# A raw query weight outside the row slots, two last expert rows weighed one by one, and an earlier second head in the last mixer

## What is computed

```
ue = peer_u[experts]
ve = peer_v[experts]
act = jax.nn.gelu(jnp.einsum('td,thkd->thk', hc, ue).astype(jnp.float32), approximate=False)
return jnp.einsum('thk,thkd->td', (g * act).astype(ve.dtype), ve)
```

```
m = jnp.maximum(jnp.max(s, axis=-1, keepdims=True), sink)
e = jnp.exp(s - m)
p = e / (jnp.sum(e, axis=-1, keepdims=True) + jnp.exp(sink - m))
o = jnp.einsum('bnkgqp,bnpkd->bnqkgd', p.astype(vb.dtype), vb)
```

## Time and profile before

| | |
|---|---|
| runs of the kernel, us | 1650.83, 1653.07, 1652.2: median 1652.2 |
| the profiled execution, us | 1650.42, its span 1648.6 |
| mean granted TensorE clock | 0.981 |
| busy share of the span | PE 91%, weight loads 66%, DVE 68%, ACT 46%, POOL 17% |
| the chain that ended last | PE 64%, DMA 18%, DVE 11%, ACT 4% |
| DMA | 443 MB, of which 268 MB are the expert rows |

### The profile page before, as it was taken

How to read it: one execution, slowest core, us unless ns; L and a number is a source line. 1 busy time by engine, 2 the same in 40 slices (tenths; PEclk the granted TensorE clock), 3 DMA queues, 4 the chain that set the end, 5 groups by cost and what they waited for, 6 DMA issues and landing times.

```text
span 1648.6 us, 18823 instructions
## 1 busy us (share of the span) xinstructions
PE 1504.9 (91%) x6882; PEld 1090.7 (66%) x6882; DVE 1121.2 (68%) x2054; ACT 753.4 (46%) x1401; POOL 284.3 (17%) x317
## 2 busy tenths in 40 slices
PE   7999999999789889788798777879999999899999
PEld 6899888888644444344353332338888889788887
DVE  6669666666877766767866876458666566866654
ACT  5444553344434444334443433235555347655532
POOL 0000000000243333334433334313000002000000
PEclk9999999999999999999999999999999999999999
DMA  6754544554599999999999999984455554135563
GB/s 241 269 179 157 176 154 153 179 181 162 217 419 421 421 421 420 421 421 409 422 421 421 403 422 421 404 346 144 153 188 195 186 198 135 52 131 195 186 191 116
DMA packets 73356, 443.04 MB, mean 269 GB/s; under 512 B 7047, under 2 KB 9359, under 8 KB 29872
## 3 DMA queue, kind: packets, MB, share of 16 engines
q0 software_dynamic: 36864, 268.45, 39.4%
q1 hardware_dynamic: 32672, 165.69, 29.6%
q10 hardware_dynamic: 3728, 7.70, 1.3%
HBM read 440.75 MB, written 2.63 MB: 269 GB/s over the span
## 4 chain that ended last, share of the span: by engine, by line
PE 64%; DMA 18%; DVE 11%; ACT 4%; issue 2%; POOL 0%; SPq 0%; DVEq 0%; ACTq 0%; POOLq 0%
PE banks L1410 24%; DMA arena<-experts,xn 18%; PE banks L1845 11%; PE banks L1433 11%; PE banks L1438 6%; DVE arena L2474 3%; PE banks L1320 3%; PE banks L1733 2%; DVE w_lo L2037 2%; PE banks L1552 1%; PE banks L1575 1%; ACT xn L1010 1%; PE banks L1344 1%; ACT xn L1014 1%; PE banks L1501 1%
## 5 line engine op out<-in xcount | busy, mean ns | idle before, releaser
L1845 PE MATMUL banks<-arena,xn 128*128 128x512 f32 x1024 | 499.1, 626 | 108.5 <-ACT xn L1014 108.2
L2037 DVE TENSOR_TENSOR w_lo<-raw,w_hi 128x2048 fp32r<-128x2048 f32 x152 | 348.0, 2290 | 198.4 <-PE banks L1410 100.5
L2474 DVE CUSTOM_DVE_ANT_0 arena<-arena,banks 128x1024 f32<-128x1024 f32 x256 | 311.7, 1218 | 191.9 <-DMA arena<-experts,xn 191.5
L1845 PEld LDWEIGHTS banks<-arena,xn 128*128 128x128 f32 x1024 | 188.7, 197 | 343.4 <-issue 172.9
L717 ACT ACTIVATE w_hi<-raw 128x2048 fp32r<-128x2048 f32 x152 | 291.1, 1918 | 234.2 <-PE banks L1410 145.7
L652 POOL DMA_INDIRECT arena<-experts,xn x256 | 252.0, 984 | 421.5 <-PE banks L1845 388.3
L1410 PE MATMUL banks<-w_hi,op 128*128 128x512 f32 x1152 | 292.7, 393 | 1.4 <-DVE op L2671 0.8
L1410 PEld LDWEIGHTS banks<-w_hi,op 128*128 128x128 f32 x1152 | 216.5, 189 | 47.7 <-issue 2.1
L1003 ACT ACTIVATE xn<-xn,stat 128x2 f32<-128x2 f32 x128 | 37.8, 295 | 378.9 <-DVE xn L2474 378.8
L1433 PE MATMUL banks<-op,w_hi 128*128 128x512 f32 x792 | 200.4, 393 | 0.0
L1433 PEld LDWEIGHTS banks<-op,w_hi 128*128 128x128 f32 x792 | 141.8, 189 | 25.9 <-issue 1.1
(11 more groups left out here) (277 smaller groups left out, 1371.6 us busy)
## 6 DMA issues: line engine op xcount, KB each, us to landing
raw<-wstream SPq DMA_DIRECT2D x152, 1024.0 KB, 5.4
arena<-experts,xn POOLq DMA_INDIRECT x256, 12.7
xn<-mem_in ACTq DMA_DIRECT2D x2, 1024.0 KB, 6.4
arena<-wstream SPq DMA_DIRECT2D x2, 1024.0 KB, 7.9
scratch<-scratch ACTq DMA_DIRECT2D x1, 1536.0 KB
x<-x_in SPq DMA_DIRECT2D x2, 512.0 KB, 4.8
arena<-scratch ACTq DMA_DIRECT2D x1, 1024.0 KB, 7.3
raw<-keys_in SPq DMA_DIRECT2D x1, 1024.0 KB, 4.7
```

The source lines that it names most:

```text
L1845: mm = pe.matmul(sums[:, n, :], diag[:, s, :], rows[:, s, D + n * CW:D + (n + 1) * CW], start=(at == 0), stop=(at == PAIRS - 1), skip_grou ...
L2037: dve.tensor_tensor(w_lo[:, n % LO, :, :], slot_of(n), w_hi[:, n % HI, :, :].bitcast(F32), ALU.subtract).then_inc(lo_ready, 1)
L2474: dve.tensor_tensor_reduce(u, u, token_rows[k // PAIRS][:, :, :], 1.0, 0.0, ALU.mult, ALU.add, dots[:, s:s + 1]).then_inc(dot_ready, 1)
```

## The change

There are five edits.

1. The fourth `pq` half is loaded into `memkv`, a buffer of 128x2048 that is `memk` and `memv` in one, which hold nothing until later. Only the third half lies in a row slot, the last. So row 6 waits for no low part, and row 7 for that of the third half instead of the fourth.
2. `weigh_rows` can weigh a single row; the last two rows, 254 and 255, are weighed one by one.
3. `add_rows(1)` begins its first half when the first of the last row's two products is done (`last_sum`), its second half when the row is.
4. In `swa` the second item is normalised directly after the first, and the low parts of both `outb` halves follow it, ahead of the maxima of the third item. `take_inverses(2)` and `memory_inverses` no longer make low parts.
5. Normalisation of the first `memb` head stands ahead of the last `take` of `swa`.

ACT gets one more call, `high_parts(LAST[("inb", 3)] + 1)`, ahead of `queries(2)`. The call that `queries(2)` makes itself asks for the same halves, and ACT's order there is unchanged.

```diff
-        extra = part((GSLOTS - EXTRA) * 2 * D, EXTRA, KC, HW)
+        extra = [part((GSLOTS - 1) * 2 * D, KC, HW), memkv.rearrange("p a b c d -> p (a b c) d")]
...
-                if SLOT[n] >= RAW:
+                if SLOT[n] == RAW:
                     sp.wait_ge(merged_lo, 4)
...
-                if GSLOTS - EXTRA <= k < GSLOTS:
-                    pool.wait_ge(lo_ready, LAST[("pq", 2 + k - (GSLOTS - EXTRA))])
+                if k == GSLOTS - 1:
+                    pool.wait_ge(lo_ready, LAST[("pq", 2)])
...
-            def weigh_rows(k):
+            def weigh_rows(k, n=2):
...
-                    weigh_rows(n * TOPK + j)
+                    if n * TOPK + j == TB * PAIRS - 2:
+                        weigh_rows(TB * PAIRS - 2, 1)
+                        weigh_rows(TB * PAIRS - 1, 1)
+                    else:
+                        weigh_rows(n * TOPK + j)
...
+                        if k == TB * PAIRS - 1 and n == 0:
+                            mm.then_inc(last_sum, 1)
...
-                    normalise(kind, i)
+                    if not (begun and i == 0 or second and i == 1):
+                        normalise(kind, i)
+                    if second and i == 0:
+                        normalise(kind, 1)
+                        second()
...
+                if after:
+                    normalise(after, 0)
                 for i in range(items - late, items):
                     take(kind, i, dst)
...
-                dve.wait_ge(row_free, GSLOTS + (tb + 1) * PAIRS)
                 for n in range(2):
+                    if tb and n == 0:
+                        dve.wait_ge(last_sum, 1)
+                    else:
+                        dve.wait_ge(row_free, GSLOTS + (tb + 1) * PAIRS)
...
-                low_parts(LAST[("inb", 3)] + 2)
                 dve.wait_ge(memory_roots, 1)
...
-                      [lambda: take_inverses(2), None, None, memory_inverses], after="memb")
+                      [lambda: query_inverses(("qr", 2), 2), None, None, memory_inverses], after="memb",
+                      second=lambda: low_parts(LAST[("inb", 3)] + 2))
```

More of the change, by code:

```diff
@@ L320, in build @@
         sub_step = part(6656, S)[0:HEADS, :]
-        extra = part((GSLOTS - EXTRA) * 2 * D, EXTRA, KC, HW)
+        extra = [part((GSLOTS - 1) * 2 * D, KC, HW), memkv.rearrange("p a b c d -> p (a b c) d")]
         def slot_of(n):
-            return raw[:, SLOT[n], :, :] if SLOT[n] < RAW else extra[:, SLOT[n] - RAW, :, :]
+            return raw[:, SLOT[n], :, :] if SLOT[n] < RAW else extra[SLOT[n] - RAW]
         keys = raw[:, SPARE, :, :].rearrange("p a (b k) -> p (a b) k", b=2)
@@ L997, in query_work @@
                     copy_scores(h)
-            def weigh_rows(k):
+            def weigh_rows(k, n=2):
                 s = k % GSLOTS
-                act.wait_ge(dot_ready, k + 2)
-                act.activation(gact[:, s:s + 2], dots[:, s:s + 2], ACT.Gelu,
+                act.wait_ge(dot_ready, k + n)
+                act.activation(gact[:, s:s + n], dots[:, s:s + n], ACT.Gelu,
                                scale=stats("ffn")[3][:, k // PAIRS:k // PAIRS + 1]).then_inc(gelu_ready, 1)
-                act.wait_ge(gelu_ready, k // 2 + 2)
-                act.wait_ge(row_free, k + 2)
-                for e in range(2):
+                act.wait_ge(gelu_ready, k // 2 + 2 + (n == 1 and k % 2))
+                act.wait_ge(row_free, k + n)
+                for e in range(n):
                     at = k % PAIRS + e
@@ L1011, in weigh_rows @@
                                    scale=weight[:, k // PAIRS, at:at + 1]).then_inc(wact_ready, 1)
[L1012 to L1013 removed]
+                act.wait_ge(wact_ready, k + n)
+                for e in range(n):
                     act.activation(diag[:, s + e, :], ident, ACT.Copy, scale=wact[:, s + e:s + e + 1])\
@@ L2225, in take, with attention @@
                                              op_hi[lo:hi, buf, d, :].bitcast(F32), ALU.subtract), key)
-            def attention(kind, items, group, lag, extra, dst, fill=(), lows=(), after=None, begun=False):
+            def attention(kind, items, group, lag, extra, dst, fill=(), lows=(), after=None, begun=False,
+                          second=None):
                 for i in range(0 if begun else min(lag, items)):
```

8 lines of the change are left out of this document (4 added, 4 removed).

## The result

The changed kernel takes 1639.06 us (median of 6 runs, 1638.35 to 1642.75) against 1651.34 us (6 runs, 1649.25 to 1653.07): ratio 0.9937, interval [0.9927, 0.9948]. That is 12.3 us less. Measured a second time, the ratio was 0.9946 [0.9932, 0.996], 9.0 us.

A forecast was written before the change was run, and what follows sets the result against it. The prediction took the expert-row stage as paced by transfers, with chains of small steps at the tail and last attention. Terms 0.9 + 2.6 + 1.9 + 0.6 = 6.0 us gave 1646.2 us; forecast range 1643.5 to 1649, 8-in-10 range 1642 to 1650.

The forecast's parts named there:

- Edit 1, 0.9 us: Start of the row stage: lost transfer falls from 5.7 to 4.8 us; term 0.9 us, bounds 0 and 5.7.
- row 10 keeps its 453.48 and row 12 its 458.83: Row stage start: these fetches stay put, as row 2's product still waits for the fourth half's low part.
- the forecast had counted 4.8: Row stage start: transfer still lost after the change, from idle of 2.3, 0.2 and 2.3 us around rows 10 to 12.
- Rival A: Row stage start: all idle goes because DVE and PE free rows 2 to 4 sooner; 1641.4 us, chance 0.10.
- Rival D: Row stage start: row 12's issue is not lengthened, its bytes start 2.1 us earlier, term 3.0; 1644.1 us, chance 0.08.
- rule of the Trainium skill: DVE and GpSimd share ports exclusively, but `tensor_tensor` does not hold up descriptor writing; row 12's issue would take 0.94 us.
- The tail, 2.6 us: End of the rows: one row's 1.85 us leaves the path, earlier adds save 0.7; bounds 1.85 and 3.3.
- The attention, 1.9 and 0.6 us: Last mixer: 1.9 us at the attention's start, bounds 0.7 and 4.5; 0.6 us at the windowed heads' end.
- 1.4 forecast: Last mixer's attention at `memory_inverses`: DVE waits about 1.4 us for POOL, with item 4's normalisation queued behind.
- bound of 0.83: End of the windowed heads: upper bound of the 0.6 us term, PE's turn having waited 0.83 us for the normalisation.
- rival C: Changed attention: pauses drop PE to 1.2 GHz; slower, 1658.2 us with 12 us of such work; chance 0.04.

The follow-up runs named there:

- slot edit: Only the fourth raw query half moved out of the row slots, on the kernel before: 1648.16 us, ratio 0.9985; run again 1644.86 us, 0.998.
- tail alone: Only single weighing of the last two rows and the early first add, on the kernel before: 1649.31 us, ratio 0.9997; run again 1648.92 us, 0.9992.
- whole without slot: The whole change without moving the fourth raw query half out of the row slots: 1643.9 us, ratio 0.9962 to the kernel before.
- later inverses: The whole change with `memory_inverses` taken two items later in the last sliding attention: 1640.18 us, ratio 0.9944 to the kernel before.
- slot and tail: Edits 1 to 3 on the kernel before, last mixer's attention unchanged, no empty ACT call: 1645.17 us, ratio 0.9972; run again 1644.9 us, 0.997.
- later start: The whole change plus 12 repeated 128x128 turns on PE in the merge at 310 us, delaying everything behind: 1640.84 us, ratio 0.9947 to the kernel before.

## Why the prediction was wrong

**Edit 1, 0.9 us, is the step that failed.** The step "row 10 keeps its 453.48 and row 12 its 458.83" took the 3.55 us of row 2's product as the product's length. It was the length at half clock: 1.88 us in the profile after. The window with clock 0.69 stood in the earlier trace rows beside it. Before the change this delay was hidden, since the gap behind row 6 covered it: rows 0 to 32 take 88.9 to 90.2 us in eight profiles, with the half clock on row 2 (three) or not (five). With the slot edit the delay is next in line. Then the stretch is 85.2 to 86.0 us in eight profiles where row 2 was not hit, and 87.8 in the slot edit's own profile where it was. So the term is 89.6 - 85.5 = 4.1 us in one kind of execution and 1.8 in the other. The slot edit run twice shows both kinds with one and the same program, 87.80 and 85.48. A delay of 1.7 us grows on the way: row 12's issue begins at 22.1 us behind row 0's dot or at 23.8, and with the slot edit the low part beside it begins at 23.3, so the issue is over at 23.0 or only at 26.4.

In the other kind the forecast's fetch times held (453.38, 458.72, 2.64 us long), and the term was still 0.9 too small. By the windows that execution lost 5 x (3 - (239 + 352 + 305) / 421) = 4.4 us of transfer where the forecast had counted 4.8, which explains half of it; the other half was not found. Rival A's time, 1641.4, comes nearest of those given, but its mechanism did not: row 2's product was not started sooner, it was shorter, and 1.6 us of transfer were still lost.

**Row 12's long issue.** Rival D said that the issue would not be lengthened, at 1644.1. That happened, and not for the reason of the rule of the Trainium skill weighed there ("SBUF — State Buffer", "Who interferes with whom"): fetches whose issue meets a DVE subtraction do last longer, 2.15 us at 445.16 beside the low part at 444.21 and 1.65 at 457.78 beside the one at 456.33. The issue was 1.7 us earlier and missed the low part. Each of the long ones ends 0.8 us behind the end of its subtraction, and one that begins ahead of the subtraction is not lengthened. It turns on hundredths: before, row 12 began 0.05 us behind the low part and took 3.04 us; in the tail alone (timeline) it began 0.04 us ahead and took 0.94.

```profile
458.76 0.94 POOL L653 DMA_INDIRECT arena<-experts,xn  x1 [1.74 <-PE banks L1850]
...
458.80 2.29 DVE L2044 TENSOR_TENSOR w_lo<-raw,w_hi 128x2048 fp32r<-128x2048 f32 x1
```

Without the slot edit a long issue cost little: the tail alone and the whole without slot have none (0.94 us for rows 12 and 13), and their stretches are 88.86 and 90.11.

**The tail, 2.6 us.** 2.61: twelve profiles with both edits have 11.61 to 11.69 us, seven with neither 14.26 to 14.28. The forecast was right in mechanism and size.

**The attention, 1.9 and 0.6 us.** 1.8 and 0.9: 222.05 to 220.23 with the fourth edit, to 219.34 with the fifth. S of item 4 gained 1.2, DVE waited 1.38 us for POOL (1.4 forecast), and later inverses showed that this wait was on the path. The fifth was not run alone: its 0.9 is the difference of these two, and lies 0.06 over its bound of 0.83. What the forecast didn't see is the clock: PE's pause of 2.41 us was taken as an argument against rival C only. The same pause stood ahead of the fall that cost 3.3 us in slot and tail, so it is also a risk of the kernel without the edit.

**What no edit gave.** 2.0 us of the 12.1 lie ahead of row 0's dot. The first fetch is at 423.3 to 425.1 us in the profiles, whatever the edits (leaving out later start, which delays it), and the two executions had different clocks far ahead of it (windows before, then after):

```profile
250.00:255.00 5.00, 5.00 (x13) 3.93 (x12) 4.97 (x4) 0.00 (x0) 0.00 (x0) 0.50 0.25 66
...
250.00:255.00 5.00, 5.00 (x20) 4.06 (x19) 4.97 (x3) 0.00 (x0) 0.00 (x0) 0.82 0.37 107
```

Over 240 to 260 us the clock was 0.83 in five profiles, whose first fetch is at 424.85 to 425.14, and 0.91 in the others, where it is at 423.29 to 424.77. Slot alone has it at 425.00 in one profile with 0.83, and at 423.71 in the other with 0.91. That part of the gain is luck. Another 0.8 lies between rows 32 and 255. The cuts that follow the edits give 4.1 + 2.6 + 2.7 = 9.4 us, ratio 0.9943, which both measured intervals hold. The sum from one pair of executions and the range around it left out that two executions differ by such amounts.

## What to carry to other kernels

A duration taken from a window with a clock below 1 is not the operation's length: before it is used as the next limit, price it at full clock and say which of the two an execution may have. As long as a wait hides a delay, the delay costs nothing; the change that removes the wait exposes it. And where single edits sum to less than the whole, cut every profile at the same marks before believing in an interaction.

## What the runs showed of the hardware

The granted clock fell to half for 3 to 7 us at a time (0.66 over 5 us in later start; 0.50 over 5 us and 0.84 over the next 5 in slot and tail). The falls on the products of rows 0 and 2 and in the attention came in or behind pauses of PE of 1.9 to 3.6 us, but not every such pause was followed by one: the slot edit's program met it on row 2's product in one execution and on row 0's in another, and filling one pause moved the fall to a later one. A pause just ahead isn't needed either: from 250 to 255 us before, the clock was 0.50 with PE busy for 5.00 of 5 us, and PE was as busy from 245 to 250.

A fetch's issue on POOL, 0.94 us, took up to 3.0 us where it began during a 2.29 us subtraction of 128x2048 on DVE: it then ended 0.8 us or a little more behind the end of that one. Begun ahead of the subtraction, it took its 0.94 us. POOL's eight slope scalings took 3.34 us with no low part beside them, 5.17 with one and 6.73 with two; the low parts themselves took 2.3 to 2.4 us.
